# The second product of the 768-token feed-forward stages as seven products of quarters

## The reference

```python
def swiglu(x, w13, w2):
    a, b = jnp.split(x @ w13, 2, axis=-1)
    return (jax.nn.silu(a) * b) @ w2

def ffn_half_step(h, g, shift, scale, gate, w13, w2):
    return h + 0.5 * gate * swiglu(modulate(rms_norm_2(h, g), shift, scale), w13, w2)
```

## Time and profile before

| | us |
|---|---|
| median of three runs | 4195.26 |
| lowest and highest | 4182.81, 4198.72 |
| span of the profiled execution | 4193.0 |
| TensorE busy in it | 3991.0 (95%) |
| VectorE busy | 2480.2 (59%) |
| ScalarE busy | 1708.2 (41%) |
| GpSimd busy | 202.8 (5%) |

### The profile page before, as it was taken

The page is one execution under the profiler, slowest core; times in us unless marked ns, Lnnn a source line. Parts: engine busy times, 40 slices in busy tenths (PEclk is TensorE's granted clock), DMA queues, the critical chain, the costliest instruction groups (busy, mean ns, idle before and its releaser), DMA issues. The chain is left out here.

```text
span 4193.0 us, 92837 instructions
## 1 busy us (share of the span) xinstructions
PE 3991.0 (95%) x40800; PEld 3568.4 (85%) x40800; DVE 2480.2 (59%) x3882; ACT 1708.2 (41%) x2992; POOL 202.8 (5%) x159
## 2 busy tenths in 40 slices
PE   6999999998999998999999999999999999989999
PEld 5777777777788887999997769999999999668998
DVE  5565665554444443756655557566576665657776
ACT  4433433342255554533333425333353333445443
POOL 0111111011000000000001110000000000120000
PEclk9999999999999999999999999999999999999999
DMA  4001010004345545112121101211212112112222
GB/s 172 19 14 28 28 28 27 27 4 160 126 170 180 180 177 220 61 71 71 61 81 54 59 31 61 72 70 61 81 53 74 65 61 81 64 58 73 105 106 81
DMA packets 99875, 337.03 MB, mean 80 GB/s; under 512 B 5009, under 2 KB 66834, under 8 KB 71826
## 3 DMA queue, kind: packets, MB, share of 16 engines
q1 hardware_dynamic: 99474, 331.09, 22.1%
HBM read 326.62 MB, written 4.46 MB: 79 GB/s over the span
## 5 line engine op out<-in xcount | busy, mean ns | idle before, releaser
L1042 PE MATMUL banks<-x_hi,w_hi 128*128 128x384 f32 (+1 forms) x2496 | 806.7, 323 | 12.6 <-ACT ffn_tiles L1172 6.3
L1043 PE MATMUL banks<-x_lo,w_hi 128*128 128x384 f32 (+1 forms) x2496 | 802.6, 322 | 0.0
L1044 PE MATMUL banks<-x_hi,w_lo 128*128 128x384 f32 (+1 forms) x2496 | 802.6, 322 | 0.0
L1149 ACT CAST w_hi<-landing_all 128x512 fp32r<-128x512 f32 x768 | 457.4, 619 | 317.0 <-DVE landing_all L1254 300.2
L1246 DVE TENSOR_TENSOR w_lo<-landing_all,w_hi 128x512 fp32r<-128x512 f32 x768 | 515.6, 684 | 49.9 <-ACT w_hi L1149 49.8
L1042 PEld LDWEIGHTS banks<-x_hi,w_hi 128*128 128x128 f32 x2496 | 471.6, 189 | 21.9 <-DVE x_lo L1352 9.5
L1043 PEld LDWEIGHTS banks<-x_lo,w_hi 128*128 128x128 f32 x2496 | 471.9, 189 | 0.4
L1044 PEld LDWEIGHTS banks<-x_hi,w_lo 128*128 128x128 f32 x2496 | 471.8, 189 | 0.0
L1043 PE MATMUL banks<-g_lo,w_hi 128*128 128x384 f32 (+1 forms) x1234 | 421.7, 342 | 0.0
L1042 PE MATMUL banks<-g_hi,w_hi 128*128 128x384 f32 (+1 forms) x1234 | 421.6, 342 | 0.0
L1044 PE MATMUL banks<-g_hi,w_lo 128*128 128x384 f32 (+1 forms) x1234 | 421.6, 342 | 0.0
(11 more groups left out here) (491 smaller groups left out, 7514.3 us busy)
## 6 DMA issues: line engine op xcount, KB each, us to landing
landing_all<-in_w SPq DMA_DIRECT2D x132, 1024.0 KB, 4.8
arena_first<-in_ada_w SPq DMA_DIRECT2D x38, 2048.0 KB, 8.6
weight_ring_first<-in_rw_pair SPq DMA_DIRECT2D x32, 512.0 KB, 5.2
landing_all<-in_w_in SPq DMA_DIRECT2D x12, 1024.0 KB, 4.8
weight_ring_first<-in_da_head SPq DMA_DIRECT2D x16, 512.0 KB, 9.7
weight_ring_first<-in_da_head SPq DMA_DIRECT2D x8, 1024.0 KB, 6.3
landing_all<-in_w_out SPq DMA_DIRECT2D x8, 1024.0 KB, 5.2
x_normed_first<-in_ada_w SPq DMA_DIRECT2D x3, 2048.0 KB, 10.9
```

What stands on the lines that cost most here:

```text
L1042: mm(o, wh, xh, start=first, stop=False, skip_group_check=onto)
L1043: mm(o, wh, xl, start=False, stop=False, skip_group_check=onto)
L1044: return mm(o, wl, xh, start=False, stop=last, skip_group_check=onto)
L1149: nc.scalar.copy(SH[:, q % RING], raw(q)).then_inc(whi.h, 1)
```

## The change

The three 768-token stages call a new function, `ffn_sevens`, a copy of `ffn` for two segments with these differences. The 512-token stage still calls `ffn`.

- A w unit of four tiles becomes two loads of seven slots, each the seven products of quarters for four output tiles: the four tiles of D_FF in two halves (inner quarters of two tiles), the output tiles in rows, the tokens in two halves of 384. Each product is made for two pairs of output tiles (ab = 0, 1), each pair member two `triple`s in a bank of its own: 12 matmuls a product, 84 a load, 168 a unit. The last unit (`last_two`, two tiles of D_FF) stays plain, now with 512 and 256 columns in place of twice 384.
- VectorE makes the four sums of weights of each of these loads in place, as in a g unit.
- After each product VectorE adds its two banks straight to the residual (`add_out`): 384 columns in one instruction where the product belongs to the first half of the tokens (P1, P2, P6, P3), 128 and 256 columns in two where it belongs to the second (P5, P7, P4).
- The gated tiles are split in pairs: two tiles are four quarters. `g_high` and `g_low` split three of them (384 and 768 columns), `g_sum` makes four sums (four chained instructions of 384 columns), `g_sums_high` and `g_sums_low` split the sums and the fourth quarter (1536 columns). These are put at 1, 2, 3, 4 and 5 products behind the end of the pair.
- The ring has 8 slots in place of 11; product n brings slot n + 5, and the splits of slots 8, 9 and 10 leave the opening. Four gated tiles are kept in place of two.
- Banks are given out by a small list (`allot`), oldest released first.
- The packed array of w2 is reordered on the host for these stages.

```diff
+        PLAIN, RING, RAW = 2, 8, 4
+        A11, A21, A12, A22, S1, S2, S4 = range(7)
+        S3 = A21
+        G11, G12, G22, GS2, GS3, GS4, GS1 = range(7)
+        P1, P2, P5, P7, P6, P4, P3 = range(7)
+        x_operand = (A11, A12, S1, S3, S2, A22, S4)
+        g_operand = (G11, G12, GS1, GS3, GS2, G22, GS4)
+        bank_of = (0, 1, 2, 0, 0, 0, 2)
+        target = ((0, 0), (0, 0), (1, 1), (1, 1), (1, 0), (0, 1), (1, 0))
+        w_order = (P1, P2, P6, P5, P7, P3, P4)
...
+            elif u < 5:
+                order += [q + P1] + held + [q + p for p in w_order[1:]] + [q + 7 + p for p in w_order]
+                held = []
...
+        splits_at, nxt = [], RING
+        for n in range(Q):
+            splits_at.append([])
+            if nxt < Q and used_up(nxt - RING) <= n + 1:
+                splits_at[-1].append(nxt)
+                nxt += 1
+            assert n + 1 == Q or order[n + 1] < nxt
...
+        banks, released = {}, [-1] * 8
+
+        def allot(key, at, until):
+            banks[key] = min((n, b) for b, n in enumerate(released) if n < at)[1]
+            released[banks[key]] = until
+
+        for n, q in enumerate(order):
+            kind, u, part, _, q0 = slots[q]
+            if q0 in sevens and part in (P1, P2, P5):
+                for ab in range(2 if kind == "w" else 1):
...
+                def second(q):
+
+                    _, c, part, _, q0 = slots[q]
+                    first, x, r = part in (P1, P2, P5), g_operand[part], q % RING
+                    pe.wait_ge(glo.h, glo.at(0, 4 * c + (3 if part in (P1, P2, P4) else 4)))
+                    pe.wait_ge(wlo.h, wlo.at(0, q + 1))
+                    for ab in range(2):
+                        b = bank_at(q, ab)
+                        if first:
+                            take_bank(b, out_done, out_no[q0 + {P1: P4, P2: P2, P5: P3}[part], ab])
+                        else:
+                            pe.wait_ge(out_done.h, out_done.at(0, out_no[q0 + {P6: P1, P7: P6, P4: P7, P3: P5}[part], ab]))
+                        for k in range(2):
+                            ins = triple(bank(b), SH[:, r, 2 * ab + k], SL[:, r, 2 * ab + k], OH[:, x, k], OL[:, x, k], k == 0 and first, k == 1, not first)
+                        ins.then_inc((first_done if ab == 0 else slot_done).h, 1)
...
+                def g_high(u):
+                    act.wait_ge(g_ready.h, g_ready.at(0, 2 * u + 2))
+                    g = raw_pair(u)
+                    if u == FT - 1:
+                        act.wait_ge(slot_done.h, slot_done.at(0, ended(begin["g", u] + P3)))
+                        for s in range(2):
+                            nc.scalar.copy(GH[:, s], SG[(u - 1 + s) % RAW]).then_inc(ghi.h, 1)
+                        return
+                    if u == 1:
+                        act.wait_ge(sums_lo.h, sums_lo.at(0, 5))
+                    if u >= 4:
+                        act.wait_ge(slot_done.h, slot_done.at(0, ended(begin["w", u // 4 - 1] + 7 + P4)))
+                    k = u % 4 // 2
+                    nc.scalar.copy(OH[:, G11, k], g[:, 0])
+                    nc.scalar.copy(OH[:, G12:G22 + 1, k], g[:, 2:4]).then_inc(ghi.h, 1)
+
+                def g_sums_high(u):
+                    act.wait_ge(g_sums.h, g_sums.at(0, u // 2 + 1))
+                    nc.scalar.copy(OH[:, GS2:GS1 + 1, u % 4 // 2], raw_pair(u)).then_inc(ghi.h, 1)
+
```

and VectorE's part:

```diff
+                def g_low(u):
+                    g, k = raw_pair(u), u % 4 // 2
+                    if u == FT - 1:
+                        for s in range(2):
+                            dve.wait_ge(ghi.h, ghi.at(0, u + s))
+                            tt(GL[:, s], SG[(u - 1 + s) % RAW], GH[:, s].bitcast(F32), ALU.subtract).then_inc(glo.h, 1)
+                        return
+                    dve.wait_ge(ghi.h, ghi.at(0, u))
+                    tt(OL[:, G11, k], g[:, 0], OH[:, G11, k].bitcast(F32), ALU.subtract)
+                    tt(OL[:, G12:G22 + 1, k], g[:, 2:4], OH[:, G12:G22 + 1, k].bitcast(F32), ALU.subtract).then_inc(glo.h, 1)
...
+                def g_sum(u):
+                    g = raw_pair(u)
+                    dve.wait_ge(glo.h, glo.at(0, u))
+                    L(tt(g[:, 3], g[:, 1], g[:, 3], ALU.add))
+                    L(tt(g[:, 1], g[:, 0], g[:, 1], ALU.subtract))
+                    L(tt(g[:, 0], g[:, 3], g[:, 0], ALU.subtract))
+                    tt(g[:, 2], g[:, 2], g[:, 0], ALU.subtract).then_inc(g_sums.h, 1)
+
+                def g_sums_low(u):
+                    k = u % 4 // 2
+                    dve.wait_ge(ghi.h, ghi.at(0, u + 1))
+                    tt(OL[:, GS2:GS1 + 1, k], raw_pair(u), OH[:, GS2:GS1 + 1, k].bitcast(F32), ALU.subtract).then_inc(glo.h, 1)
+
+                def add_out(q, ab):
+                    _, _, part, n, q0 = slots[q]
+                    x, h = target[part]
+                    x, at = x + 4 * loads[n][2] + 2 * ab, 512 * bank_at(q, ab) - h * H
+                    if part in (P2, P7, P3):
+                        dve.wait_ge(out_done.h, out_done.at(0, out_no[q0 + {P2: P1, P7: P5, P3: P6}[part], ab]))
+                    for c, c0, cn in in_half[h]:
+                        xs = X[:, x, c0:c0 + cn]
+                        ins = stt(xs, PS[:, at + c0:at + c0 + cn], half[:, x, c:c + 1], xs, ALU.mult, ALU.add)
+                    ins.then_inc(out_done.h, 1)
...
+                    elif kind == "w":
+                        dve.wait_ge(first_done.h, first_done.at(0, product_no[q] + 1))
+                        add_out(q, 0)
+                        done()
+                        add_out(q, 1)
...
+                        gated(u, 1, X3)
+                    if n - 2 in pair_end:
+                        g_low(pair_end[n - 2])
+                    if pair_end.get(n - 3, FT) < FT - 1:
+                        g_sum(pair_end[n - 3])
+                    if pair_end.get(n - 5, FT) < FT - 1:
+                        g_sums_low(pair_end[n - 5])
+                    if n == begin["g", PLAIN] - 1:
+                        x_sum_low(4)
+                    if n:
+                        for q in splits_at[n - 1]:
+                            split(q)
```

and the calls and the packing:

```diff
             m = lambda j: mods[:, 48 + 72 * layer + 8 * j:48 + 72 * layer + 8 * j + 8, :]
             gain = lambda n: K.par(n)[:, 8 * layer:8 * layer + 8]
-            K.ffn(layer, 1, BOTH, m, gain("g_ffn1"), f"{layer}_1", mix_first(layer))
+            K.ffn_sevens(layer, 1, m, gain("g_ffn1"), f"{layer}_1", mix_first(layer))
             K.mix_buffers(f"mix{layer}")
             K.mixing(layer, last, gain("g_mix"), m(3), m(4), m(5), ffn_first(2, layer))
-            K.ffn(layer, 2, segs, lambda j: m(j + 6), gain("g_ffn2"), f"{layer}_2", [] if last else ffn_first(1, layer + 1))
+            if last:
+                K.ffn(layer, 2, LATENT, lambda j: m(j + 6), gain("g_ffn2"), f"{layer}_2", [])
+            else:
+                K.ffn_sevens(layer, 2, lambda j: m(j + 6), gain("g_ffn2"), f"{layer}_2", ffn_first(1, layer + 1))
         K.final(K.par("g_final"))
...
-        fours = w2[:, 0:20].reshape(DEPTH, 5, 4, P, 2, 4, P).transpose(0, 1, 4, 3, 5, 2, 6).reshape(DEPTH, 10, P, 2048)
+        fours = w2[:, 0:20].reshape(DEPTH, 5, 2, 2, P, 2, 2, 2, P).transpose(0, 1, 5, 4, 3, 7, 6, 2, 8).reshape(DEPTH, 10, P, 2048).copy()
+        if n == 2:
+            fours[DEPTH - 1] = w2[DEPTH - 1, 0:20].reshape(5, 4, P, 2, 4, P).transpose(0, 3, 2, 4, 1, 5).reshape(10, P, 2048)
```

401 lines of the change are left out of this document (added).

## The result

The changed kernel takes 4236.64 us, the median of four runs (4232.33 to 4240.63), against 4195.66 for the kernel before (four runs, 4182.81 to 4198.72). The ratio is 1.0106, 95% interval [1.0090, 1.0122]: 1.06% slower, where the forecast was 0.5% slower (4216). Sign and place of the loss were right; its size was twice what the sum gave.

What follows compares the result with a forecast made beforehand. TensorE's matmuls were taken to bound the 768-token stages if VectorE delivers in time. Stalls of 29.3 us less 1.4 and 20.8 give +7.1 a stage, +21.3 in all: 4216 us, range 4200 to 4236 (4160 to 4242 leaves out 2 in 10).

Steps and rivals of the forecast that it cites:

- the rule L - 1.84: At each P6: lateness in us, L being how long after a product's end VectorE finishes that product's queue.
- What bounds it, and what is removed: 768-token stages last as long as their matmuls; 120 fewer a stage at 0.173 us save 20.8 us, 62.4 in three.
- What VectorE pays: VectorE's prices: 15.1 us a w load against TensorE's 14.5, 12.2 against 14.5 in a g unit.
- The rival of dear residual instructions: In the w units: 384 columns at 0.58 to 0.67 us give 4229 to 4254 us; chance 14%.
- P6 is where it shows: P6, third product of its unit, waits for VectorE's split: about 0.5 to 1.95 us late in steady units.
- Its 0.16 for TensorE's start: At a late P6: 0.16 us lost between the releasing result and TensorE's regular matmuls.
- The first unit of seven: Behind the opening, with slots 8 to 10 no longer split there: P6 late by 3.0 us.
- The fifth w unit: Priced like the other w units: first P6 late by 1.95 us, second by 1.2, together 3.15.
- TensorE's clock: All stages: stalls far shorter than the work between them were taken as harmless to the faster clock.
- the rival: Thirty w stalls each bring one product at the 1.2 GHz level: 62 us more, 4278 us; chance 3%.
- Costed at nothing: ScalarE's extra splits and high parts, banks, and loads in the stages: no delay charged.
- 91% by the forecast: VectorE's average load over w and g units, w units over their limit and g units under it.

Runs made afterwards that it cites:

- e5: The changed kernel with slots 8, 9 and 10 split in the opening again, the ring still at 8: 4227.38 us, ratio 1.0100.
- e14: e6 with P6 and P7 exchanged in the order of ring slots: 4181.25 us, ratio 0.9971.
- e1: The kernel before, plain w units kept, with a ring of 8 slots in the 768-token stages and no splits of slots 8 to 10 in the opening: 4235.35 us.
- e3: The changed kernel with VectorE's split of a product moved ahead of its wait for the next product: 4191.59 us, ratio 1.0004.
- e4: The changed kernel with the list of splits taking every slot free at a product, not one: 4192.78 us, ratio 1.0002.
- e13: The changed kernel with P6 and P7 exchanged in the order of ring slots: 4218.88 us, ratio 1.0061.
- e6: e5 with VectorE splitting ahead of its wait in g units and at P1 of w units, behind the residual elsewhere: 4185.96 us, ratio 0.9994.
- e11: e6 with the w units' residual instructions cut to 32 columns: 4143.54 us, ratio 0.9891.
- e12: e6 with the second seven products of w units 1 to 4 moved behind the next g unit: 4188.92 us, ratio 0.9998.
- e9: e6 with the low part of S3 made one product later and ScalarE's cast of S3 behind its splits: 4190.92 us, ratio 1.0000.

## Why the forecast had the sign and missed the size

The 8.7 us a stage that the sum missed have three causes of like size: the lower clock behind two waits, which was put at nothing (3.2), the delay of each late P6, which the rule L - 1.84 made too small (3.3 with the fifth w unit), and the opening, whose order I had wrong (2.2).

- **What bounds it, and what is removed: right.** 40440 matmuls, 0.173 us each, as forecast.
- **What VectorE pays: right.** 858 splits, 440 sums, 67% busy. 384 columns of residual last 609 ns against 0.61, two cost 1.05 us of pitch (0.53 each), 128 and 256 together 0.65 against 0.63. The rival of dear residual instructions, whose range (4229 to 4254) holds the result, is not what happened; it would have given the right time for a wrong reason.
- **P6 is where it shows: right.** 30 of the 34 late products of the first stage are P6, released by `w_lo`. The rule "late by L - 1.84" was 0.07 to 0.17 short at each, 3.2 us a stage (table). Its 0.16 for TensorE's start was too small by 0.07 in the g units and by 0.02 in the w units: that is all of the shortfall in g units after g units and a part of it elsewhere; the rest stays open.
- **The first unit of seven: mis-ordered**, 6.8 us against 3.0. I charged the removed splits of slots 8 to 10 to VectorE's queue behind the plain units but let the opening end sooner by what they had cost. It didn't: they had lain in waits for ScalarE (e5). P1 comes 1.4 late, which I had not seen at all, P6 waits 3.7, and the lower clock behind it adds 1.6.
- **The fifth w unit: right but for the clock**, 4.9 against 3.15. I took five alike. In the fifth the low parts of the last two gates, 768 columns each, fall into the first load, and the wait moves to its second P6 (2.3 us); in sum the unit waits 3.3 us as the others do, and the lower clock adds 1.6.
- **TensorE's clock: wrongly dismissed**, 3.2 against nothing. I took every stall here as harmless from one wait of 1.44 us. Behind the gap of 3.85 us (and behind one of 2.4 at the fifth w unit) ten matmuls come at the 1.2 GHz level, 0.32 us apart. A stretch laid over them alone has the granted clock 0.50 (last line, third figure from its end), though the mean of the long stretch still reads 1.00:

```profile
1748.02 0.41 PE L1549 MATMUL banks<-x_hi,w_hi 128*128 128x384 f32 x1 [3.51 <-DVE w_lo L1765]
...
1748.66 0.52 PE L1549 MATMUL banks<-x_hi,w_hi 128*128 128x384 f32 x1
1748.98 0.52 PE L1550 MATMUL banks<-x_lo,w_hi 128*128 128x384 f32 x1
...
1748.60:1751.90 3.30, 3.30 (x13) 3.30 (x12) 3.23 (x6) 0.12 (x1) 0.00 (x0) 0.50 0.00 0
```

  Ten times 0.15 is 1.5 us, and the matmuls at either end add 0.1. That came twice in the first and in the third stage; in the second it was 17 matmuls in the opening (2.5 us) and none at the fifth w unit. It was a surcharge on the two largest waits, not one on all thirty w stalls as the rival priced it. From the Trainium skill (TensorE: Matmul & The Clock Gate, What's actually happening) I had concluded that stalls far shorter than the work between them are harmless; these rows don't bear that out for waits above 2 us.
- **Costed at nothing: held.** No wait for ScalarE or a load in the stages; one of 0.4 us for a bank in the fifth w unit. With VectorE's order mended the banks do become what TensorE waits for in the w units (e14).
- **Which cause is whose** came from the experiments: the short ring with its list of splits costs by itself what the change costs (e1); in the g units each of three edits is enough to end P6's stalls, the split ahead of the wait (e3), several slots at once (e4) and P6's slot one earlier (e13, which brings others at P1), so VectorE had the time there and did the split too late; in the w units order and load share it, and once the order is mended load is what is left (e6 against e11). That VectorE's average (91% by the forecast) left room did not help where a split stood behind a wait (e12).
- **Open**: the rest of the P6 rule's shortfall; how the opening's last 3 to 4 us, which moved from P6 to P1 in e9 and e14, could be hidden; what the seven products would give with 11 slots, or with e4's list in e14.

## What to carry to other kernels

Before a fast algorithm is paid for with buffer slots, price the slots: shorten the ring in the old kernel and time that alone, and see whether the list that fills the ring uses every slot as soon as it is free. In a strictly ordered queue behind a short ring, put the work whose consumer is next ahead of any wait, and give slots in the order in which they are consumed; here these two edits and the restored opening turned 1.06% slower into 0.3% faster. Work that fills an engine's waits is free where it stands: moving it makes the place it leaves no shorter.
